# Two modulation rows loaded as pairs of feature blocks, with normalisation made pair by pair beside the first dense products

## The reference, cut to what matters

```
mod = silu(c) @ w_ada + b_ada                  # (1024) @ (1024, 6*1024), once for c, once for c_ctx
shift1, scale1, gate1, shift2, scale2, gate2 = split(mod, 6)
h = rmsnorm(x, norm1_w) * (1 + scale1) + shift1
z = h @ w_in                                   # first dense products
...                                            # short convolutions, gated delta rule, w_out
x = x + gate1 * y
h = rmsnorm(x, norm2_w) * (1 + scale2) + shift2
x = x + gate2 * conv_glu(h)                    # w_up, 3x3 convolution, w_down
y = rmsnorm(x, final_norm_w)
```

## Time and profile before

| | |
|---|---|
| median of 3 runs | 1575.22 us (1572.38 to 1576.77) |
| span of the profiled execution | 1575.5 us |
| TensorE busy | 1520.2 us, 96% of the span |
| VectorE, ScalarE, GpSimd busy | 932.3, 481.8 and 405.4 us |
| first dense product starts | 52.21 us |
| first product of the third block (the pair is done) | 83.20 us |
| mean granted TensorE clock | 0.989 of full |

### The profile page before, as it was taken

The page is one execution under the profiler, slowest core; times in us unless marked ns, Lnnn a source line. Parts: engine busy times, 40 slices in busy tenths (PEclk is TensorE's granted clock), DMA queues, the critical chain, the costliest instruction groups (busy, mean ns, idle before and its releaser), DMA issues.

```text
span 1575.5 us, 24058 instructions
## 1 busy us (share of the span) xinstructions
PE 1520.2 (96%) x9744; PEld 1466.3 (93%) x9744; DVE 932.3 (59%) x1398; ACT 481.8 (31%) x902; POOL 405.4 (26%) x204
## 2 busy tenths in 40 slices
PE   5899999999999999999999999999999999999997
PEld 1788999999998999998999999999999999999996
DVE  2753453569997895328875276436734673476257
ACT  4331254231157784225221212122202210221024
POOL 0011111561134452320331132113311321232120
PEclk9799999999999999999999999999999999999999
DMA  9453323632426467110111111111111111111103
GB/s 347 193 195 141 108 73 117 190 111 78 139 73 189 125 204 293 54 54 15 41 42 51 43 41 41 41 41 41 41 49 47 41 40 41 42 41 41 40 1 120
DMA packets 74112, 142.60 MB, mean 91 GB/s; under 512 B 19212, under 2 KB 44372, under 8 KB 72340
## 3 DMA queue, kind: packets, MB, share of 16 engines
q1 hardware_dynamic: 70116, 131.38, 24.5%
q10 hardware_dynamic: 3456, 7.87, 1.3%
q0 software_dynamic: 432, 1.77, 0.3%
HBM read 120.34 MB, written 20.65 MB: 89 GB/s over the span
## 4 chain that ended last, share of the span: by engine, by line
PE 90%; DVE 4%; DMA 2%; ACT 2%; issue 2%; POOL 0%; SPq 0%; DVEq 0%; ACTq 0%; POOLq 0%
PE ps L2410 52%; PE ps L2412 26%; PE ps L1197 5%; PE ps L2349 2%; DMA araw<-wts 2%; PE ps L2359 1%; PE ps L1170 1%; PE ps L2618 1%; DVE fa L2243 1%; PE ps L2519 1%; PE ps L2478 0%; PE ps L1142 0%; DVE X L2130 0%; DMA q<-q_d 0%; PE ps L2696 0%
## 5 line engine op out<-in xcount | busy, mean ns | idle before, releaser
L2410 PE MATMUL ps<-hH,wH 128*128 128x384 f32 x1680 | 567.5, 338 | 8.5 <-DVE hL L1847 3.6
L2412 PE MATMUL ps<-hL,wH 128*128 128x384 f32 x1680 | 562.8, 335 | 0.0
L1323 POOL TENSOR_TENSOR wL<-raw,wH 128x1024 fp32r<-128x1024 f32 x93 | 226.3, 2433 | 893.7 <-ACT wH L1521 893.2
L2410 PE MATMUL ps<-hH,wL 128*128 128x384 f32 x1680 | 382.7, 335 | 0.0
L2410 PEld LDWEIGHTS ps<-hH,wH 128*128 128x128 f32 x1680 | 316.5, 188 | 16.4 <-issue 13.8
L1521 ACT ACTIVATE wH<-raw 128x1024 fp32r<-128x1024 f32 x99 | 105.1, 1062 | 722.0 <-PE ps L2410 720.9
L2412 PEld LDWEIGHTS ps<-hL,wH 128*128 128x128 f32 x1680 | 316.5, 188 | 0.0
L2243 DVE SCALAR_TENSOR_TENSOR fa<-G,cst,fa 128x1024 f32<-128x1024 f32 x176 | 297.1, 1688 | 15.4 <-DVE fa L2240 0.6
L2410 PEld LDWEIGHTS ps<-hH,wL 128*128 128x128 f32 x1680 | 300.6, 188 | 0.0
L2410 PE MATMUL ps<-pH,wH 128*128 128x384 f32 x528 | 179.3, 340 | 4.1 <-DVE pL L2267 1.9
L2130 DVE SCALAR_TENSOR_TENSOR X<-ps,mod,X 128x384 f32<-128x384 f32 x138 | 70.5, 566 | 188.8 <-PE ps L2410 188.8
(11 more groups left out here) (332 smaller groups left out, 1856.9 us busy)
## 6 DMA issues: line engine op xcount, KB each, us to landing
raw<-wts SPq DMA_DIRECT2D x103, 512.0 KB, 3.3
araw<-wts SPq DMA_DIRECT2D x48, 512.0 KB, 6.1
X<-xT SPq DMA_DIRECT2D x8, 1152.0 KB, 15.4
kv<-tok_d SPq DMA_DIRECT2D x16, 512.0 KB, 4.8
tok_d<-stage ACTq DMA_DIRECT2D x18, 256.0 KB, 2.1
gb<-grow_d SPq DMA_DIRECT2D x18, 256.0 KB, 3.9
q<-q_d SPq DMA_DIRECT2D x17, 256.0 KB, 5.6
y<-X SPq DMA_DIRECT2D x8, 384.0 KB, 2.4
```

Source lines behind the costliest of these rows:

```text
L1323: nc.gpsimd.tensor_tensor(weight(1, u4), raw[:, u4 % RAW, :], weight(0, u4).bitcast(F32), ALU.subtract).then_inc(s["wl_ready"], 1)
L2410: last = M(out, lhs, rh[:, c], start=(k == 0 and not lo), stop=(lo and k == kts - 1))
L2412: M(out, lhs, rl[:, c], start=False, stop=False)
```

## The change

**Loads.** The whole of X, the ones and the first weight unit are loaded first. Rows 0 and 1 of the modulation come behind them in 16 loads of 512 KB each, ordered by four pairs of feature blocks: loads 4p to 4p+3 bring 256 output features (blocks 2p and 2p+1) of rows 0 and 1, from all 1024 input features. One load takes four input blocks, so a partition gets four pieces of 1 KB where it got one of 4 KB. The second pair has four slots of its own, `araw2`, which lie where `hH[4]` to `hH[7]` will be written. Weight units 1, 2 and 3 stand behind loads 3, 11 and 15.

**TensorE.** The sums over features now come first and add the last square with three more matmuls. `feature_units(p)` has 16 matmuls of 256 columns in all four quarters of the array's columns; `feature_turn(p)` has four matmuls. Units and turn of pair 0 stand ahead of the first pair of blocks; the units of pairs 1, 2 and 3 stand ahead of steps k = 0, 1 and 3, and their turns between the two products of those steps.

**ScalarE.** `pair_rows(p)` copies a pair's rows: pair 0 between Ln and Exp, pairs 1, 2 and 3 ahead of `hH` of blocks 1, 2 and 4. The first weight unit is rounded before Ln.

**VectorE.** The addition at L1863 goes. `pair_mod(p)` makes shift and scale of a pair ahead of its first block; the order of `norm_apply` is now pair by pair: u, u, hL, hL. The `wL` of the second weight unit comes after the first `hL`.

Counts and waits of the later modulation rows are renumbered; their work and order stay. The diff, cut to its core:

```diff
+FEATS = 4
+N_PART = 4 * FEATS
...
-    sel = np.stack([((r // Q) % 2 == j) & (r % Q == k) for j in range(2) for k in range(2)], 1).astype(np.float32)
+    sel = np.stack([((r // Q) % 2 == j) & (r % Q == k) for j in range(2) for k in range(2)]
+                   + [r % Q == k for k in range(2)], 1).astype(np.float32)
...
+    araw2 = place("araw2", [P, ARAW, D], F32, blk(2))
...
-    def ada_bank(m):
-
-        return 5 if m == 1 else 6
+    ADA_PS = 6
+
+    def ada_slot(a):
+
+        return araw2[:, a % ARAW, :] if ARAW <= a < 2 * ARAW else araw[:, a % ARAW, :]
+
+    def ada_landed(eng, a):
+
+        if ARAW <= a < 2 * ARAW:
+            eng.wait_ge(s["ada_second"], 16 * ARAW)
+        else:
+            eng.wait_ge(ada_in[a % ARAW], (a // ARAW + (0 if a >= ARAW else 1)) * 16)
...
+            def feature_load(a):
+
+                p, r, half = a // 4, a // 2 % 2, a % 2
+                if a >= 3 * ARAW:
+                    sp.wait_ge(s["ada_used"], a - ARAW + 1)
+                elif a >= 2 * ARAW:
+                    sp.wait_ge(s["ada_used"], a - 2 * ARAW + 1)
+                src = wts[KT * r + 4 * half:KT * r + 4 * half + 4, :, 256 * p:256 * p + 256].rearrange("k p n -> p k n")
+                sem = s["ada_second"] if ARAW <= a < 2 * ARAW else ada_in[a % ARAW]
+                sp.dma_start(ada_slot(a).rearrange("p (k n) -> p k n", k=4), src).then_inc(sem, 16)
...
-            ada_load(0)
-            for q in range(3):
-                ada_load(q + 1)
+            for q in range(4):
                 x_load(q)
             sp.dma_start(cst[:, ones:ones + P], const[:, ones:ones + P]).then_inc(s["ones_in"], 16)
-            x_load(3)
+            load(N_ADA, 0, 0)
+            for a in range(4):
+                feature_load(a)
+            load(N_ADA + 1, 1, 0)
             for a in range(4, 12):
-                ada_load(a)
-            load(N_ADA, 0, 0)
+                feature_load(a)
+            load(N_ADA + 2, 2, 0)
             for a in range(12, 16):
-                ada_load(a)
-            for w in range(1, RAW):
-                load(N_ADA + w, w, 0)
+                feature_load(a)
+            load(N_ADA + 3, 3, 0)
...
+            def pair_rows(p):
+
+                act.wait_ge(s["ada_used"], 4 * p + 4)
+                if p >= 2:
+                    act.wait_ge(s["modps_ready"], p - 1)
+                A(modrow[:, p % 2, :], ps[:, ADA_PS, :], ACT.Copy).then_inc(s["modrow_ready"], 1)
...
-            def norm_rstd(k, rs, side):
+            def norm_rstd(k, rs, side, between):
 
                 for n in range(NT):
                     act.wait_ge(s["st_done"], NT * k + n + 1)
                     last = A(rs[:, n * TW:n * TW + TW], bank3(side, n), ACT.Ln, scale=1.0 / D, bias=biases[:, 0:1])
                 astep.inc(last)
+                between()
                 act.wait_ge(s["act_step"], astep.value())
                 A(rs[:], rs[:], ACT.Exp, scale=-0.5).then_inc(s["rstd_ready"], 1)
...
-                act.wait_ge(s["mod_ready"], 3)
                 for b in range(KT):
+                    if b in (1, 2, 4):
+                        pair_rows((b + 2) // 2)
                     act.wait_ge(s["u_ready"], 8 * k + b + 1)
...
-            ada_rows(0)
-            norm_rstd(0, rstd, 0)
-
-            def high(u, u4, i):
-
-                act.wait_ge(raw_in[u4 % RAW], landed(u4, i))
-                A(weight(0, u4), raw[:, u4 % RAW, :], ACT.Copy).then_inc(s["wh_ready"], 1)
-
             high(0, 0, 0)
-            ada_rows(1)
+            norm_rstd(0, rstd, 0, lambda: pair_rows(0))
+
             high(1, 1, 0)
...
+            def pair_mod(p):
+
+                dve.wait_ge(s["modps_ready"], p + 1)
+                both = slice(2 * p, 2 * p + 2)
+                by_row = lambda ap: ap.rearrange("p (r b) k -> p r b k", r=2)[:, :, both, :]
+                V.tensor_tensor(by_row(mod[:, 0:2 * KT, :]),
+                                by_row(ps[:, 7, 0:4 * KT].rearrange("p (b k) -> p b k", k=2)),
+                                by_row(cst[:, C_BADA:C_BADA + 2 * KT].unsqueeze(2).broadcast_to([P, 2 * KT, 2])),
+                                ALU.add).then_inc(s["mod_ready"], 1)
+                dve.wait_ge(s["mod_ready"], 2 * p + 1)
+                V.scalar_tensor_tensor(sc1[:, both, :], mod[:, KT + 2 * p:KT + 2 * p + 2, :], 1.0,
+                                       cst[:, C_N1 + 2 * p:C_N1 + 2 * p + 2].unsqueeze(2).broadcast_to([P, 2, 2]),
+                                       ALU.add, ALU.mult).then_inc(s["mod_ready"], 1)
+                dve.wait_ge(s["mod_ready"], 2 * p + 2)
...
+                pair_mod(0)
                 u_of(0)
                 for b in range(KT):
-                    if b + 1 < KT:
+                    if b + 1 < KT and b % 2 == 0:
                         u_of(b + 1)
-                    if b == 0:
-                        add_bias(0, 1, 2, 3)
-                    if b == 1:
-                        dve.wait_ge(s["wl_ready"], 1)
...
+                    if b == 0:
+                        dve.wait_ge(s["wl_ready"], 1)
+                        dve.wait_ge(s["wh_ready"], 2)
+                        V.tensor_tensor(wL[:, 1, :], raw[:, 1, :], wH[:, 1, :].bitcast(F32),
+                                        ALU.subtract).then_inc(s["wl_ready"], 1)
+                    if b + 1 < KT and b % 2:
+                        pair_mod(b // 2 + 1)
+                        u_of(b + 1)
...
-            dve.wait_ge(s["sq_last"], NT)
-            dve.wait_ge(s["sq_used"], 6)
-            V.tensor_tensor(ss[:], ss[:], sq[:, 1, :], ALU.add).then_inc(s["ss_full"], 1)
-            add_bias(1, 2, 1, 1)
-            scale_of(sc1, 1, C_N1)
-            dve.wait_ge(s["mod_ready"], 2)
...
+            def feature_units(p):
+
+                if p:
+                    pe.wait_ge(s["modrow_ready"], p)
+                for a in range(4 * p, 4 * p + 4):
+                    r, half = a // 2 % 2, a % 2
+                    ada_landed(pe, a)
+                    for q in range(4):
+                        last = M(ps[Q * q:Q * q + Q, ADA_PS, 256 * r:256 * r + 256], scT[:, 4 * half + q, :],
+                                 ada_slot(a)[:, 256 * q:256 * q + 256], start=(half == 0), stop=(half == 1))
+                    last.then_inc(s["ada_used"], 1)
+
+            def feature_turn(p):
+
+                pe.wait_ge(s["modrow_ready"], p + 1)
+                if p:
+                    pe.wait_ge(s["mod_ready"], 2 * p)
+                for r in range(2):
+                    for b in range(2):
+                        o = 16 * r + 2 * (2 * p + b)
+                        last = M(ps[:, 7, o:o + 2], modrow[:, p % 2, 256 * r + P * b:256 * r + P * b + P],
+                                 cst[:, C_IND + 4:C_IND + 6], start=True, stop=True)
+                last.then_inc(s["modps_ready"], 1)
...
-            for a in range(KT + 1):
-                ada_unit(a)
             pe.wait_ge(s["ones_in"], 16)
-            pe.wait_ge(s["ss_full"], 1)
-            for n in range(NT):
-                M(bank3(0, n), mat("ones"), ss[:, n * TW:n * TW + TW], start=True, stop=True).then_inc(s["st_done"], 1)
-            for a in range(KT + 1, KT + 5):
-                ada_unit(a)
-            turn(0)
-            for a in range(KT + 5, 2 * KT):
-                ada_unit(a)
-            pe.wait_ge(s["mod_ready"], 1)
-            turn(1)
-            pe.wait_ge(s["mat_in"], 32)
-            pe.wait_ge(s["mod_ready"], 3)
...
+            stats_part(0, ss, lambda n: sq[:, 1, n * TW:n * TW + TW], 0, range(NT))
+            feature_units(0)
+            feature_turn(0)
...
             def first_pair(k):
+                if k in (0, 1, 3):
+                    feature_units((k + 3) // 2)
...
-            model_pair(0, 0, first_pair)
+            for k in range(KT):
+                first_pair(k)
+                for o in range(2):
+                    if k == 0:
+                        pe.wait_ge(s["wl_ready"], o + 1)
+                    last = product_step(o, k, KT, w_of(o), h_of)
+                    if o == 0 and k in (0, 1, 3):
+                        feature_turn((k + 3) // 2)
+                    if k == KT - 1:
+                        last.then_inc(s["blk_done"], 1)
+            pe.wait_ge(s["mat_in"], 32)
```

More of the change, by code:

```diff
@@ L49 @@
 C_IND = C_ALOG + 2 * H
-C_MAT = C_IND + 4
+C_MAT = C_IND + 6
 MATS = ["ident", "ones", "UI", "LI", "US", "LS"]
@@ L1419, in ada_rows @@
                 act.wait_ge(s["ada_used"], 8 * m + 8)
-                if m >= 2:
-                    act.wait_ge(s["modps_ready"], m - 1)
-                A(modrow[:, m % 2, :], ps[:, ada_bank(m), :], ACT.Copy).then_inc(s["modrow_ready"], 1)
+                if m >= 4:
+                    act.wait_ge(s["modps_ready"], FEATS + m - 3)
+                else:
+                    act.wait_ge(s["modps_ready"], FEATS)
+                A(modrow[:, m % 2, :], ps[:, ADA_PS, :], ACT.Copy).then_inc(s["modrow_ready"], 1)
+            def pair_rows(p):
```

(30 more changed lines are left out.)

9 lines of the change are left out of this document (3 added, 6 removed).

## The result

The changed kernel took 1562.58 us (1559.65 to 1566.66, 6 runs) where the kernel before took 1573.89 (6 runs): the ratio of the runs compared is 0.9919, 95% interval 0.9902 to 0.9935, or 12.7 us (10.2 to 15.4) off; the medians alone differ by 11.3 us. The forecast was 7.7 us off and a range down to 1563.5.

What follows compares the result with a forecast made beforehand. The prediction took the start to be bound by loading 13.1 MB. First product at 36.6 plus 38.4 for the first pair of blocks plus 0.5 gave 75.5 against 83.2 us: 7.7 off, 1567.5 us, range 1563.5 to 1574.5.

Steps and rivals of the forecast that it cites:

- pair 1 in at 32.7 us: Start: loads in 1 KB pieces run at 312 GB/s, so the second pair of feature blocks is loaded at 32.7 us.
- VectorE's low part at 36.0: Before the first dense product: VectorE finishes the low part of block 0 at 36.0 us.
- the 1.9 us for the low clock in the first step: First pair of blocks: its first step begins at half clock and loses 1.9 us, as before the change.
- Last of X in at 16.7, squares summed at 19.2: Start: X is loaded at 16.7 us, 5.1 us earlier; last squares and VectorE's last addition end at 19.2.
- Six sums 6.6 us: TensorE's six matmuls with the ones: four at half clock, two at full, 5.2 + 1.4 us, done at 25.9.
- First product at 36.6: The first dense product starts at 36.6 us, 15.6 us earlier than before.
- 0.5 us for hand-overs: Allowance of 0.5 us for hand-overs between engines, which the walk otherwise counts at nothing.
- the head that I gave (75.5): Third block starts at 75.5 us instead of 83.2, 7.7 us off, all of it reaching the end.
- slow pieces: Loads in short pieces run at only 239 GB/s; 1569.7 us, chance 0.10.
- the low clock beyond step 0: First pair of blocks: half clock lasts through pair 2's units, 1570.7 us, or step 1, 1573.9; chance 0.15 short of slower.
- Rival 4: Full clock from the units of pair 1 on, 2.5 us more gained, 1565.0 us; chance 0.10.
- The claim that the gain arrives at the end: Behind the third block's start TensorE runs without a gap, so what that start gains, the end gains.

Runs made afterwards that it cites:

- the second comparison: The changed kernel timed and profiled once more with no edit, against the kernel before: 1565.25 us, ratio 0.9933.
- p512: The changed kernel with a host layout making the pieces of its 16 loads of rows 0 and 1 512 bytes long: 1562.45 us in one run.
- warm: The changed kernel with 14 unread matmuls ahead of the sums over features and 8 behind the turn of pair 0: 1557.34 us, ratio 0.9878.
- contig: The changed kernel with rows 0 and 1 laid out by the host so each load is one 4 KB piece per partition: ratio 0.9950.
- warm_early: The changed kernel with only 14 unread matmuls, ahead of the sums over features: 1586.95 us in one run.
- before again: The kernel before, unedited, profiled a second time: first product 52.01 us, third block 83.07 us; its medians beside the experiments were 1575.2 to 1576.5 us.
- x_first: The kernel before with the four loads of X and the ones ahead of all units of w_ada: 1577.9 us in one run.
- all_ahead: The changed kernel with units and turns of pairs 1, 2 and 3 all ahead of the first dense product: 1576.43 us in one run.
- contig_fill: The kernel `contig` with nine unread matmuls between the units of pair 1 and the first dense product: ratio 0.9940.
- contig_warm_fill: The kernel `contig` with unread matmuls: 14 before the sums, 4 behind pair 0's turn, 5 before the first dense product: 1558.03 us, ratio 0.9886.
- add_dve: The changed kernel with the last square added by VectorE again and three matmuls with the ones instead of six: 1565.21 us in one run.
- pad216: The changed kernel with 216 instead of 128 short waits at the head of TensorE's program: 1568.79 us, ratio 0.9959.

## Why the prediction was wrong

The walk had the right steps, and five terms of its sum were too large, all to the same side. Those that failed with most weight are the two that set the first product, pair 1 in at 32.7 us (29.95) and VectorE's low part at 36.0 (34.0), and the 1.9 us for the low clock in the first step (0.6). The time fell below the range by 0.9 us; the second comparison, with a median of 1565.25, would have lain within it.

- **Last of X in at 16.7, squares summed at 19.2.** X was in by 15.0 and TensorE began at 17.93. I took the landing of the old order and subtracted four units at 410 GB/s. The queue had moved 7.67 MB by 21.84 us in the old order and 5.23 by 15.01 in the new, which is 0.34 MB more than four units, and it moved 415 GB/s from 5 to 10 us where it had moved 362. With X in earlier VectorE's additions became the chain: five in a row, one every 1.46 us. So of 1.7 us 1.3 came through to the sums; the loads behind X had all of it.
- **Six sums 6.6 us.** They took 6.1 and 5.5 us in the two profiles: I had put four of them at the half-clock price, 5.2 us, and three ran so, in 4.13 and 3.57. 0.5 and 1.1 us. With this `rstd` and VectorE's first low part were done 1.9 to 2.0 us before the walk had them.
- **The short pieces at 312 GB/s, pair 1 in at 32.7.** It was in at 29.95, 1.7 us of the 2.75 by the earlier X, the rest by the rate, 348 GB/s. The straight line through the mixed packets of the earlier trace rows is what mis-sized the rate: the queue was not full there (52.6%), and packets of all sizes are in that mean. The row of the Trainium skill (DMA: Bandwidth & Descriptors, the table at its head) by which 512 B are enough for line rate is not borne out either: 290 GB/s at 512 bytes and 350 at 1 KB against 410 at 4 KB. Neither chain decides alone. With VectorE's as walked, the first product would have moved by 0.5 us; with pair 1 as walked it would have moved by no more, as `p512` shows: pair 1 in at 32.54, first product at 36.10.
- **First product at 36.6.** At 34.08 and 33.69, by the three terms above: 2.5 and 2.9 us.
- **1.9 us lost to the clock in the first steps.** The first step with its turn took 4.9 us where the walk had 6.1; at full clock, in `warm`, it took 4.2. So 0.6 us were lost, not 1.9: 1.2 us. I carried the loss of the old start over, where TensorE had been idle for 3.6 us before the first product. In the changed kernel the units of pair 1, slow as they are, end just before it and bring the clock up. `contig`, in which they end 4.45 us before it, took 7.8 us: a loss of 3.5.
- **0.5 us for hand-overs**: none.

Together 2.5 + 1.2 + 0.5 = 4.2 us, the whole difference between the head that I gave (75.5) and 71.3. The rest of the pair, from the units of pair 2 on, was 32.3 us in the walk and took 32.4 and 32.0; the units at 1.93 and the turns at 0.95 were right to 0.1 us, and so was that step 3 waits for little: pair 3's units took 2.25 us there, 0.3 more than pair 2's.

Of the rivals, slow pieces and the low clock beyond step 0 didn't come. Rival 4, faster still, came nearest in its number only. Its mechanism, full clock for the units of pair 1, wasn't there (they took 3.64 us), and that its 2.5 us are the 2.5 us by which the first product was early is chance. The claim that the gain arrives at the end held: in two profiles each, the tail takes 1492.3 and 1492.1 us before, 1490.5 and 1493.4 after.

## What to carry to other kernels

Order work by when the first bulk work can start, not by operand: here a quarter of two operands is enough to start, and the products cover the loading of the rest; loading the input first gained nothing without that. Give TensorE's clock a place in the walk: small work that ends right before the bulk work is worth more than work that ends early, and a faster load that only makes an idle gap can cost 3 us at the mark behind it. And where a kernel has a noise of 3 us, compare a mark in the profile near the change, not the end.

## What the runs showed of the hardware

**Falls of the clock amid full work.** In every profile the granted clock falls to 0.50 for some 3 us at a few fixed places of the program, although TensorE has no gap to speak of there. This is the kernel before, behind 18 matmuls of 16 columns (L2487):

```profile
195.00:197.00 2.00, 2.00 (x10) 2.00 (x9) 1.97 (x3) 0.81 (x2) 0.00 (x0) 0.69 0.84 296
197.00:199.00 2.00, 2.00 (x8) 2.00 (x8) 1.00 (x2) 0.00 (x0) 0.00 (x0) 0.50 0.25 97
```

The places are the same in almost all (some 110 us behind the third block, and near 475, 580, 620, 750 and 1525 us), but which of them fall differs; only `warm_early` has others, from 890 us on. The table parts the tail of every profile. "Lost to the clock" is 10 us times what the granted clock lacks to 1 in each stretch of 10 us, up to 1452 us behind the third block. "Gaps" are TensorE's waits for nothing but its own issue (below). "Rest" is the tail less the two.

| kernel | tail, us | lost to the clock | gaps | rest |
|---|---|---|---|---|
| before, before again | 1492.3, 1492.1 | 6.8, 6.8 | 3.4, 3.4 | 1482.1, 1481.9 |
| changed, again | 1490.5, 1493.4 | 6.8, 8.6 | 3.6, 3.1 | 1480.1, 1481.7 |
| `x_first` | 1491.5 | 6.8 | 3.0 | 1481.7 |
| `all_ahead` | 1492.7 | 8.5 | 3.3 | 1480.9 |
| `contig` | 1490.8 | 6.8 | 3.1 | 1480.9 |
| `p512` | 1486.9 | 3.4 | 2.5 | 1481.0 |
| `contig_fill` | 1495.7 | 6.4 | 6.0 | 1483.3 |
| `warm` | 1486.2 | 3.4 | 0.4 | 1482.4 |
| `warm_early` | 1512.6 | 17.0 | 13.2 | 1482.4 |
| `contig_warm_fill` | 1486.3 | 5.1 | 0.4 | 1480.8 |
| `add_dve` | 1490.9 | 6.8 | 3.3 | 1480.8 |
| `pad216` | 1493.0 | 3.4 | 7.4 | 1482.2 |

The tails differ by 26 us, the rests by 3.2. So the two columns account for nearly all that differs behind the third block, the 26 us of `warm_early` included. One fall costs 1.7 us, and two to five of them an execution (more in `warm_early`) are a large part of the spread of the runs: of the changed kernel's first six, the slowest had a granted clock of 0.991 and the four fastest 0.994. It is also why `p512`, with a head 2 to 3 us later, had a time as good as the changed kernel's. The fall at 190 us came in both profiles of the kernel before and in neither of the changed kernel's, but it did in `x_first` and, among the changed kernel's variants, in six of nine, with `contig` and `warm`; so it isn't tied to the old or the new text of the program.

**Code loading.** The queue that loads instructions had 51 packets of 16 KB in the two kernels with 22 or 23 idle matmuls, and 86 or 87 in all others:

```profile
q8 instruction: 87, 1.43, 0.4%
```

```profile
q8 instruction: 51, 0.84, 0.2%
```

(the changed kernel, and `warm`). The packets that are missing are those of the loop over groups: from 750 to 1500 us these two have 6 packets, all others 42 or 43. Behind the third block, TensorE waits for nothing but its own issue for 3.4 us in 5 places before, 3.6 in 5 in the changed kernel, 13.2 in 9 with 14 idle matmuls at the head (`warm_early`), 7.4 in 9 with 88 more waits, 6.0 in 9 in `contig_fill`, and 0.4 in one place in `warm`. That one place is in all of them; the others lie between passes of the loop, and there `warm` has none. The passes of the loop lie 700 us behind the edit. That the position of the code is the cause is likely, since plain waits change the gaps; which position is good isn't shown. Of what `warm` has over the changed kernel in the tail, 4.3 and 7.2 us by the two profiles, 3.4 and 5.2 are fewer falls and 3.2 and 2.7 are fewer gaps; the rest takes back 2.3 and 0.7.
